# Gated feed-forwards with seven block products per pair of weight chunks, and the third weight in three pieces

## The reference, cut to what matters

```
def swiglu_half(x, w1, w3, w2):
    return 0.5 * ((jax.nn.silu(x @ w1) * (x @ w3)) @ w2)

for l in range(DEPTH_2):
    x = layer_norm(ALPHA * x + swiglu_half(x, ffn1_w1[l], ffn1_w3[l], ffn1_w2[l]), ln1_g[l], ln1_b[l])
    ...
    x = layer_norm(ALPHA * x + mix, ln2_g[l], ln2_b[l])
    x = layer_norm(ALPHA * x + swiglu_half(x, ffn2_w1[l], ffn2_w3[l], ffn2_w2[l]), ln3_g[l], ln3_b[l])
```

## Time and profile before

| | us |
|---|---|
| median of 3 runs | 2810.04 (2809.3 to 2814.3) |
| span of the profiled execution | 2808.3 |
| the median less that span: start and end of the launch around it | 1.7 |
| TensorE busy | 2738.2 (98%) |
| VectorE, ScalarE, GpSimd busy | 1178.4, 1103.8, 884.5 (42%, 39%, 31%) |

### The profile page before, as it was taken

The page is one execution under the profiler, slowest core; times in us unless marked ns, Lnnn a source line. Parts: engine busy times, 40 slices in busy tenths (PEclk is TensorE's granted clock), DMA queues, the critical chain, the costliest instruction groups (busy, mean ns, idle before and its releaser), DMA issues.

```text
span 2808.3 us, 48030 instructions
## 1 busy us (share of the span) xinstructions
PE 2738.2 (98%) x19908; PEld 2253.3 (80%) x19908; DVE 1178.4 (42%) x1482; ACT 1103.8 (39%) x1363; POOL 884.5 (31%) x357
## 2 busy tenths in 40 slices
PE   7999999999999999989999999999999999999997
PEld 6778877888888888787888888888888777888886
DVE  5756564432222344564422234223153563622315
ACT  6576564223222246552422234222235553422224
POOL 3344444221112534261111253111644362111154
PEclk9999999999999999999999999999999999999998
DMA  5121122222222332101222332222433201222242
GB/s 200 51 83 61 61 91 76 90 99 98 100 94 105 138 124 79 61 33 46 75 105 90 106 143 98 105 90 92 147 114 105 76 3 47 75 103 91 90 148 107
DMA packets 36820, 259.69 MB, mean 92 GB/s; under 512 B 4112, under 2 KB 4160, under 8 KB 6464
## 3 DMA queue, kind: packets, MB, share of 16 engines
q1 hardware_dynamic: 34848, 249.66, 25.0%
q0 software_dynamic: 1824, 7.93, 0.8%
HBM read 255.41 MB, written 2.16 MB: 92 GB/s over the span
## 4 chain that ended last, share of the span: by engine, by line
PE 89%; DVE 4%; issue 2%; POOL 2%; ACT 2%; DMA 0%; ACTq 0%; DVEq 0%; POOLq 0%
PE ps L2493 53%; PE ps L1983 6%; PE ps L1926 6%; PE ps L2659 4%; PE ps L2714 3%; PE ps L1975 3%; PE ps L2538 2%; PE ps L2076 1%; PE ps L2061 1%; PE ps L2047 1%; POOL wl L1525 1%; PE ps L2587 1%; PE ps L1092 1%; PE ps L2645 1%; DVE sqa L2356 1%
## 5 line engine op out<-in xcount | busy, mean ns | idle before, releaser
L1525 POOL TENSOR_TENSOR wl<-raw,wh 128x2048 fp32r<-128x2048 f32 x116 | 533.1, 4595 | 604.8 <-ACT wh L2205 565.2
L2493 PE MATMUL ps<-xh,wh 128*128 128x512 f32 x1584 | 620.6, 392 | 0.0
L2493 PE MATMUL ps<-xl,wh 128*128 128x512 f32 x1584 | 616.8, 389 | 0.0
L2493 PE MATMUL ps<-xh,wl 128*128 128x512 f32 x1584 | 616.4, 389 | 0.0
L2205 ACT ACTIVATE wh<-raw 128x2048 fp32r<-128x2048 f32 x224 | 427.6, 1909 | 400.8 <-PE ps L2493 306.5
L2323 DVE TENSOR_TENSOR wl<-raw,wh 128x2048 fp32r<-128x2048 f32 x116 | 293.8, 2533 | 483.4 <-ACT wh L2205 481.4
L2166 POOL TENSOR_TENSOR hl<-hf,hh 128x1024 f32 x44 | 105.9, 2406 | 859.1 <-ACT hh L2220 859.1
L2493 PEld LDWEIGHTS ps<-xh,wh 128*128 128x128 f32 x1584 | 297.3, 188 | 71.2 <-issue 8.6
L2493 PEld LDWEIGHTS ps<-xh,wl 128*128 128x128 f32 x1584 | 297.4, 188 | 61.8
L2493 PEld LDWEIGHTS ps<-xl,wh 128*128 128x128 f32 x1584 | 297.4, 188 | 60.7
L2493 PE MATMUL ps<-hh,wh 128*128 128x512 f32 x704 | 276.8, 393 | 1.9 <-POOL wl L1525 1.6
(11 more groups left out here) (409 smaller groups left out, 4419.8 us busy)
## 6 DMA issues: line engine op xcount, KB each, us to landing
raw<-stream SPq DMA_DIRECT2D x232, 1024.0 KB, 4.8
btw<-bias_rows POOLq DMA_DIRECT2D x2, 1536.0 KB, 9.1
x<-x_in SPq DMA_DIRECT2D x4, 512.0 KB, 5.0
x<-x_in POOLq DMA_DIRECT2D x2, 1024.0 KB, 8.8
out<-x SPq DMA_DIRECT2D x4, 512.0 KB, 2.6
sgp<-sg POOLq DMA_DIRECT2D x2, 640.0 KB, 4.1
cst<-consts SPq DMA_DIRECT2D x1, 1108.0 KB, 10.5
c<-bias_consts SPq DMA_DIRECT2D x1, 1024.0 KB, 14.5
```

The costliest lines, as they stand in the source:

```text
L1525: nc.gpsimd.tensor_tensor(wl[:, p, :], raw[:, p, :], wh[:, p, :].bitcast(F32), ALU.subtract).then_inc(s["chunk_lo"], 1)
L2493: mm = te.matmul(dst, wslice(w, k), r(k), start=(start and m == 0), stop=(stop and m == len(steps) - 1))
```

## The change

Pair 0 of each feed-forward stays as it was. For the other 10 pairs, a pair is taken as one matrix of 512 outputs by 1024 inputs and cut into four quadrants of 256 by 512; x is cut into four quadrants of 512 features by 256 tokens. Seven products of such blocks, of 2 tiles x 4 K tiles x 3 = 24 matmuls of 256 tokens each, replace eight. They run in the order A11, S2, A12, S3, S1, A22, S4. A11, A12, A22 are quadrants of the weights; S1 to S4 are sums and differences of them, which VectorE makes (`quad_sum`), as it makes four such sums T of x's quadrants at the start of every feed-forward (`x_sum`). ScalarE rounds each of the seven (`hi`); the low part is made by VectorE for S2, S3, S4 and by GpSimd for A11, A12, S1, A22 (`low_by`). The high and low parts of seven blocks go round in five places (a quarter of `wh` and `wl` each, and `wh4`, `wl4`). The products are put together as follows: A11's is copied out of PSUM by ScalarE (`prod1`), A12's is added to it in PSUM; VectorE adds S2's to the copy (U2), then S3's (U3), then S1's (C22, half of the hidden tiles, at 256 tokens), A22's (C21) and S4's (C12), and multiplies the two halves by the silus (`gated`). TensorE waits for U2 before S3, for U3 before A22 and for C22 before S4, since these go on in the same banks.

The hidden tiles are kept for four pairs only: after pairs 0 to 3, 4 to 7 and 8 to 10 the third weight's 8, 8 or 6 K tiles for these are multiplied for all 8 tiles of the outcome (`down_tiles`; 24, 24 and 18 matmuls for a tile, 528 in all as before), and VectorE adds the outcome to x after each piece. Sums, shift and squares for the norm stand in the last piece. The stream has 34 chunks for a feed-forward where it had 38, in four buffers (`raw`, `rawf`). The feed-forward is written out instead of looped. Some semaphores are merged.

The core of the diff, without the tables of indices and of loads:

```diff
+PIECES = ((0, 1, 2, 3), (4, 5, 6, 7), (8, 9, 10))
+A11, S2, A12, S3, S1, A22, S4 = range(7)
+RING = 5
...
+def low_by(q):
+
+    kind, m, n = QUADS[q]
+    if kind == "pair":
+        return "dve" if n in (S2, S3, S4) else "pool"
+    return "dve" if (n % 2 if m < 2 else n == 1) else "pool"
...
+            def quad_rest(l, w, q):
+                pool.wait_ge(*hi_ready(l, w, q))
+                c = slice(0, quad_cols(q))
+                gp.tensor_tensor(quad_part(q, True)[:, c], quad_source(q)[:, c], quad_part(q, False)[:, c].bitcast(F32), ALU.subtract).then_inc(s["quad_lo_pool"], 1)
...
+                ac.activation(exp_root[:, :], cols[:, 0:1], ACT.Silu)
+                act.wait_ge(s["x_parts"], l * 24 + w * 16 + 8)
+                hi(0)
+                for m in range(3):
+                    x_sum(m)
+                hi(1)
+                hi(2)
+                act.wait_ge(s["chunk_used"], n0 + 1)
+                ac.activation(silu_t[:, :, :], ps[:, 0:2, :], ACT.Silu).then_inc(evac[0], 1)
+                act.wait_ge(s["chunk_used"], n0 + 2)
+                x_sum(3)
+                hi(3)
+                hi(4)
+                hidden_round(0)
+                for q in range(QN):
+                    kind, m, n = QUADS[q]
+                    last = kind == "pair" and m == PIECES[piece_of(m)][-1]
+                    if kind == "pair" and n == A11:
+                        act.wait_ge(s["quad_used"], g0 + q + 1)
+                        if m > 1:
+                            act.wait_ge(*pair_step(l, w, m - 1, C12))
+                        ac.activation(product1[:, :, :].rearrange("p a b -> p (a b)"), ps[:, bank_of(m), :], ACT.Copy).then_inc(s["product_act"], 1)
+                    if kind == "pair" and n == A12:
+                        silu(m, 0)
+                    if q + RING < QN:
+                        hi(q + RING)
+                    if kind == "pair" and n == S4:
+                        silu(m, 1)
+                        if last:
+                            hidden_round(m)
+                    if kind == "pair" and n == A11 and m - 1 in PIECES[piece_of(m)] and m > 1:
+                        hidden_round(m - 1)
...
+                squares(l, w, (4, 5), evicted)
+                act.wait_ge(s["quad_used"], g - 1)
+                round_chunk(l, after, 0)
                 squares(l, w, (6,), evicted)
-                round_chunk(n + 14, 0)
                 root_table(l)
...
+                        product_done(i, A11)
+                        quad_sum(i, S4)
+
+                        product_done(i, S2)
+                        dve.wait_ge(*pair_acted(l, w, i, 1))
+                        add(i, 1, sum2[:, :, :], product1[:, :, :])
+                        if f:
+                            quad_sum(f, S3)
+
+                        quad_rest(q + S4)
+                        if f:
+                            quad_sum(f, S1)
+
+                        product_done(i, S3)
+                        add(i, 1, sum3[:, :, :], product1[:, :, :])
+                        if f:
+                            quad_sum(f, S2)
+
+                        product_done(i, S1)
+                        summed(i, U3)
+                        dve.wait_ge(s["hidden_lo"], l * 22 + w * 11 + i + 1)
+                        add(i, 2, hidden[:, :, 256:512], sum3[:, :, :])
+                        quad_rest(q + 7 + 1)
...
+                if o == A12:
+                    pe.wait_ge(*pair_acted(l, w, i, 1))
+                if o in (S3, A22, S4):
+                    pe.wait_ge(*pair_step(l, w, i, {S3: U2, A22: U3, S4: C22}[o]))
...
+                pe.wait_ge(*low_ready(l, w, q))
...
+                for m in range(2):
+                    for k in range(4):
+                        c = slice(256 * k + P * m, 256 * k + P * m + P)
+                        for n, (low, r) in enumerate(((False, rh), (False, rl), (True, rh))):
+                            mm = te.matmul(ps[:, bank, 256 * m:256 * m + 256], quad_part(q, low)[:, c], r[:, k, :], start=(fresh and m + k + n == 0),
+                                           stop=(m == 1 and k == 3 and n == 2), skip_group_check=True)
+                mm.then_inc(s["quad_used"], 1)
```

More of the change, by code:

```diff
@@ L222 @@
 SIGNALS = {
-    "mean_matrix_set": "1 / D is written",
-    "apart_pe": "nobody waits for these three: such an increment stands between a wait and",
-    "apart_dve": "an instruction that is to carry no wait of its own",
-    "apart_pool": "(the same, on GpSimd)",
-    "columns_set": "VectorE has set the constant columns",
+    "apart": "nobody waits for it: such an increment stands between a wait and an instruction that is to carry no wait of its own",
+    "columns_set": "VectorE has set 1 / D, the constant columns, and the columns behind the last group's maxima and sums",
     "consts_in": "constants",
@@ L235 @@
     "x_in3": "tiles 6 and 7",
-    "rms_columns": "mean squares by token",
+    "rms_columns": "mean squares by token, then the reciprocals over all partitions",
     "h_low": "the lo part of a tile of h that VectorE makes",
-    "rrms_wide": "the reciprocals over all partitions",
-    "rel_in": "relative position table",
-    "first_params_in": "first block's parameters",
+    "first_params_in": "first block's parameters and its relative position table",
     "layer_params_in": "a layer's parameters",
@@ L247 @@
     "chunk_used": "TensorE is through with a chunk",
+    "quad_hi": "ScalarE has rounded a quadrant of a pair of chunks, or of a sum of such, or a tile's weights of a down stage, or a sum of x's quadrants",
+    "quad_lo_dve": "the lo part of one of these that VectorE makes, T1 and T2 first",
+    "quad_lo_pool": "and of one that GpSimd makes, T4 second, T3 fourth",
+    "quad_used": "TensorE is through with a quadrant's product, or with a tile of a down stage",
+    "quad_sum": "sums of a pair's quadrants: S3, S1, S2, S4; those of x's, T1, T2, T4, T3, stand behind pair 1's S1",
+    "product_act": "ScalarE's steps of a pair: the first product in SBUF, silu of C11, then of C12",
+    "pair_sum": "VectorE's: U2, U3, C22, C21, the hidden tiles' first 256 tokens, C12, the other tokens; and tiles of x after an earlier piece's down stage",
     "x_parts": "a tile of x's parts are written",
@@ L263 @@
     "x_again": "x loaded once more, for the residual",
-    "half_hi": "ScalarE has rounded the first half of the chunk after a norm",
     "ln_columns": "mean and mean square by token",
@@ L343 @@
     "stat_ps": "maxima, then sums as rows in PSUM",
-    "stat_pad": "columns behind the last group's maxima and sums are set",
     "stat_step": "VectorE's steps of the shared maxima, the denominators and the factors",
@@ L2307, in _ @@
                 squares(l, 1, (7,), evicted)
-                half(n + 3, 0)
-                half(n + 3, 1)
+                half(l, OFF_OUT + 5, 0)
+                half(l, OFF_OUT + 5, 1)
                 norm(l, 1)
-                up(l, 1, 0, OFF_UP2, True)
-                with act.Fori(1, UP // 2) as i:
-                    up(l, 1, i, OFF_UP2)
-                down(l, 2, OFF_DN2)
+                ffn(l, 1)
+                down_end(l, 2, "down2", PER)
         @block.vector
@@ new lines, in down_part @@
+            def down_part(l, w, m, d, ks, first, last):
+                q = PIECE_AT[m] + d
+                bank = (3, 4 if m < 2 else 5)[d % 2]
+                for a, k in enumerate(ks):
+                    for n, (low, r) in enumerate(((False, hh), (False, hl), (True, hh))):
+                        mm = te.matmul(ps[:, bank, :], quad_part(q, low)[:, k * P:(k + 1) * P], r[:, k, :], start=(first and a == 0 and n == 0), stop=(last and a == len(ks) - 1 and n == 2))
+                if last:
+                    mm.then_inc(s["quad_used"], 1)
@@ L2577, in down, with ffn @@
+            def ffn(l, w):
+                for m, pairs in enumerate(PIECES):
+                    for i in pairs:
+                        if i:
+                            for o in range(7):
+                                product(l, w, i, o)
+                    down_tiles(l, w, m)
                 busy(4)
-                pe.wait_ge(evac[1], n_evac(l, 1, off) + KT)
+                pe.wait_ge(evac[1], n_evac(l, 1, ("down1", "down2")[w]) + KT)
             def shift(l, w):
```

648 lines of the change are left out of this document (465 added, 183 removed).

## The result

The changed kernel takes 2901.74 us (median of 4 runs, 2900.25 to 2903.49), the one before 2812.17 in the same comparison (4 runs, 2809.3 to 2821.13): a ratio of 1.0304, 95% interval 1.0282 to 1.0326. It is slower, as forecast, but by 90 us where the sum said 53, and above the upper end of the range, 2890. The profiled spans are 2898.6 and 2808.3, so the 90.3 us between them can be looked for in the two traces.

A forecast was written before the change was run, and what follows sets the result against it. TensorE, busy 98% of the span, was taken as the bound. Columns -65, middle pairs +38, other pairs +5, starts +52, ends +16 and clock +7 sum to +53: 2810 + 53 = 2863 us, range 2785 to 2890.

The forecast's parts named there:

- Columns: Products of pairs 1 to 10: 168 matmuls of 256 columns at 119.8 ns replace 96 at 226.7; -65 us in 40 pairs.
- The rival of shorter distances: 256-column matmuls come at 113 ns, winning 1.08 us more in 24 pairs that no turn holds up: 2837 us; chance 0.02.
- The shared turn: In the pairs, VectorE's two-SBUF-operand operations and GpSimd's exclude each other, 20.1 us of turns in 20.13; +38, other pairs +5.
- the 16 pairs named: Pairs 2, 5, 6 and 9 of each feed-forward: stalls of 2.2 us ahead of A22 and 0.2 ahead of S3; +38 us.
- the turns are never in the way: Rival: VectorE and GpSimd each run at their own pace, without exclusion: 2767 us; chance 0.14.
- VectorE keeps them: Rival: VectorE keeps the turn while its queue is full, so middle pairs lose some 0.5 us: 2805 us; chance 0.16.
- The start: Pair 1 of each feed-forward: S2 waits 5.3, A12 2.6, the pair is 13.7 us longer (10.5 in the first); +52 us.
- the worked pair: Pair 1 worked out behind x's last low part: 33.8 us where 20.1 would do, +13.7, with S2 stalling 5.3 and A12 2.6.
- The end: Last piece of each feed-forward: tile 6's square is summed late behind GpSimd's low part, net 4.1 us each; +16 us.
- The clock: Half speed behind stalls at S2 and A22 of pair 1 and the last tile: +7 us, between 0 and 14.
- worse by the clock: Rival: every stall of 2.2 us in a middle pair drops the clock, A22 runs at half speed: 2890 us; chance 0.07.
- other pairs: Pairs 3, 4, 7, 8 and 10: U3 comes in time, some 0.3 us lost; with waits at the pieces +5 us.

The follow-up runs named there:

- e3_short: Kernel after, with GpSimd's low parts of A11, A12, S1 and A22 in the pairs cut to 64 columns instead of 1024: 2815.06 us, ratio 1.0015.
- e10_halves: Kernel after, with each of GpSimd's low parts in a feed-forward made by two instructions of half the columns: 2862.17 us, ratio 1.0184.
- e1_order: Kernel after, with VectorE's sums S1 and S2 of the following pair put behind the additions U3 and C22: 2919.89 us, ratio 1.0377.
- e12_clock: Kernel after, with spare matmuls ahead of nearly every wait of TensorE's in a feed-forward: 2880.74 us, ratio 1.0239.
- e4_spare: Kernel after, with spare matmuls ahead of TensorE's waits for S2 and A22 in pair 1 and A22 in pair 2: 2895.52 us, ratio 1.0293.
- e5_dve: Kernel after, with VectorE making nearly all of GpSimd's low parts in the pairs, its order written anew: 2828.3 us, ratio 1.0053.

## Why the sum was short

*Columns, right.* 0.120 us a matmul, 64.2 us. (The rival of shorter distances priced 24 pairs without a turn in the way; pair 1 is among them, so they are 20, and 22 us instead of 26.)

*The shared turn, right, and slightly better than worked out.* U3 is late by turns in just the 16 pairs named, 1.96 and 0.25 us where 2.2 and 0.2 stood, and e3_short shows what the exclusion costs: without GpSimd's turns in the pairs 87 us are gone. The Trainium skill (SBUF — State Buffer, Terms) says that VectorE and GpSimd share a pair of ports, which is held for the whole instruction while the other engine blocks fully. This trace agrees at every overlap shown, and so does e10_halves. What I read too kindly is what follows from a sum of 20.1 us of turns in a pair of 20.13: ahead of e1_order I took the stall ahead of A22 as a fault of the order, and putting two sums back only moved it. The two rivals below the time of before fall: that the turns are never in the way with e3_short, that VectorE keeps them with the rows above, where GpSimd gets in between VectorE's operations that stood in line.

*The start, right in size.* 45.7 of waits for 52. S2 waits 5.2 and 5.5 in the second and fourth feed-forward (5.3 worked out), and S3 and A22 1.8 and 4.1, which is 5.9 where the worked pair has 5.8 left for both. The third was taken as alike and isn't: S2 waits 7.6 there. A12's 2.6 are 0.2 to 0.4, because S2's time at 1.2 GHz covers most of them, as the prediction's step on the clock had said; with S2 at full clock, in e12_clock, A12 waited 1.8 in three of the four.

*The end, right in mechanism, too small.* The sum of the square of tile 6 was held behind GpSimd's low part, for 4.70 us. Worked out were 4.1 us for each end, measured are 29.5 / 4 = 7.4, of which some 1.8 are the clock; taking the order alone back gave 24 us, not 16. The last matmul of tile 7's first half starts at 1015.30, the sums of the squares at 1021.25: 5.9 us, since VectorE's sum starts right behind the start of the low part (1016.50, 1016.02) and sits through all of it.

*The clock, the step that failed.* I had 7 us, at most 14, for A22 and half a tile. The trace has 27 in the first halves and 7 at the ends, and with work in the waits 21 came back, 19 of them inside the feed-forwards. A22 of pair 1 was foreseen at up to 1.7 (1.6 to 2.2 in the trace); not foreseen were A22 of pair 2, 1.6 in each feed-forward behind a wait of only 1.96 (6.4 in all), A11 of pair 1 in the third feed-forward (2.3), and 0.1 at the first matmuls behind every wait (4.5). S2's 6.2 at 1.2 GHz had been put at nothing because A12 would wait anyway; they stand here in place of A12's waits, 10.4 worked out and 1.4 measured. The rival "worse by the clock" had that mechanism, for all 16 middle pairs; it came in four of them in this execution and in six others in that of e4_spare.

*Outside, a term that was missing.* The stretch ahead of pair 1 of the first feed-forward grew by 3.7 us, the three between a feed-forward's end and the next one's pair 1 by 4.0, 4.0 and 1.3, and the tail not at all. I had looked only at what the diff does to the feed-forwards. In the kernels of the experiments, with much the same code there, these stretches come to 1450 to 1462 us, where the one profile of the kernel before has 1444.6, so chance alone is unlikely. Some of it is chance: in the first stretch TensorE falls to 1.2 GHz at 115 and at 473 us (granted clock 0.50 from 116 to 118 and from 474 to 476), far ahead of the feed-forwards. The profiles of before, e1_order and e5_dve don't have this, and reach pair 1 at 665.5, 666.1 and 666.3 us where after has 669.2. Between the layers it is TensorE's wait ahead of A11, behind the engines' return to the start of the loop (below). The cause of the others is open.

So the clock in the first halves is 20 us over its term, the ends 13, the outside 13 and the columns 1; the starts, middle and other pairs are 10 under theirs, 6 of it S2's time in place of A12's. That is the 37 us by which the sum was short.

## What to carry to other kernels

Add up the turns of two engines that exclude each other as if they were one engine, and set the total against the time of the loop. Where it filled the loop here, giving the work to the faster of the two won 73 us, and cutting the slower one's instructions in half 40, while the one reordering that was tried inside the pairs lost 18. A new wait of TensorE's can have a second price in the clock behind it (1.4 to 2.3 us behind each of the nine waits of 2.6 us and more, 1.6 behind four of the sixteen of 1.96), which belongs in the sum with its own line. Work in the waits (spare matmuls) got 21 us of that price back, with the waits still there.

## What was not expected of the hardware

What the exclusion costs hangs on the length of an instruction too, and not on the work alone: GpSimd's 192 low parts of 1024 columns made as 384 of 512 (and 16 of 768 as 32 of 384) gave 40 us. VectorE's busy share of 62% includes time in which it was started and blocked: the same instructions make 56% with GpSimd's short.

The return to the start of the layers' loop takes longer in the kernel with more code written out. ScalarE's first instruction of the second layer stands 3.69 us behind the last of the first layer (2.61 in the kernel before), and GpSimd's load of the layer's parameters, issued at 1776.62, comes 4.1 us behind the end of ScalarE's last one at 1772.5, which it waits for (1730.49 and 1.1 before). ScalarE's first rounding, GpSimd's low part and TensorE's A11, at 1785.37, follow from that load. ScalarE in order of time, then GpSimd:

```profile
1771.23 1.32 ACT L2570 ACTIVATE x<-zn,pkt 128x512 f32<-128x512 f32 x2
1776.23 1.28 ACT L2506 ACT_TABLE_LOAD   x1 [3.69 <-issue]
```

```profile
1776.62 0.59 POOL L2435 DMA_DIRECT2D pkt<-pk  x1 [18.86 <-issue]
```

Code loaded while running is 163 packets and 2.67 MB on the page of after, 108 and 1.77 MB before; that the one is the cause of the other was not tried.
